# Splitting the next head's first weight block into halves across VectorE and SyncE, and reordering ScalarE and VectorE work in a hybrid decoder block

## What is computed

```python
# one chip core computes all of it; 528 tokens = 16 meta tokens + 512, width 1024, 8 heads of 128
u    = rmsnorm(h, norm_g)
proj = u @ w_in                                  # (528 x 1024) @ (1024 x 10240)
hq, hf, hi, hz, aq, ak, av, az, ga, gb = split(proj)
f    = lb + (1 - lb) * sigmoid(hf);  kA = 1 - f
oA   = hgrn2_chunked(hq, log(f), kA, hi)         # gated linear recurrence, per head
yA   = (rmsnorm(oA) * silu(hz)) @ w_branch_a
oB   = diff_attention(rope(aq), rope(ak), av, lam)  # two causal softmaxes, one subtracted, per head
yB   = (rmsnorm(oB) * (1 - lam_init) * silu(az)) @ w_branch_b
h    = h + (sigmoid(ga) * yA + sigmoid(gb) * yB) @ w_out
out  = rmsnorm(h, final_g)                       # the meta tokens dropped
```

## Time and profile before

| what | us |
|---|---|
| median of 3 runs (734.7 to 736.45) | 734.8 |
| the profiled execution's own time | 735.62 |
| span of the profiled execution | 733.7 |
| PE busy | 707.5 (96%) |
| DVE busy | 531.7 (72%) |
| ACT busy | 363.7 (50%) |
| POOL busy | 112.9 (15%) |

### The profile page before, as it was taken

One profiled execution on the slowest core, in us unless ns is written; L12 is line 12 of the kernel. 1 busy time (PEld: TensorE's weight loads), 2 busy tenths in 40 slices (PEclk: granted clock), 3 DMA queues, 4 the chain that ended last, 5 costly groups with the idle time before them and its releaser, 6 DMA issues.

```text
span 733.7 us, 14433 instructions
## 1 busy us (share of the span) xinstructions
PE 707.5 (96%) x4953; PEld 651.0 (89%) x4953; DVE 531.7 (72%) x1240; ACT 363.7 (50%) x739; POOL 112.9 (15%) x134
## 2 busy tenths in 40 slices
PE   2999999999999999999999999999999999999995
PEld 2998999999899899999989999989989988888884
DVE  4899878788768777878877877887688872735352
ACT  5454653655464565376455455536566562222232
POOL 2011211221121122121112112112111000000000
PEclk9999999999999999999999999999999999999998
DMA  7355545557546554655754755565677553325102
GB/s 271 115 130 130 130 130 157 130 114 179 107 114 186 129 129 130 162 126 119 177 111 107 194 117 131 144 156 132 143 201 201 188 175 111 99 102 201 58 14 102
DMA packets 36243, 101.86 MB, mean 139 GB/s; under 512 B 4050, under 2 KB 4452, under 8 KB 36212
## 3 DMA queue, kind: packets, MB, share of 16 engines
q1 hardware_dynamic: 21492, 68.29, 26.9%
q0 software_dynamic: 14400, 32.51, 25.4%
q10 hardware_dynamic: 320, 0.66, 0.3%
HBM read 66.84 MB, written 2.10 MB: 94 GB/s over the span
## 4 chain that ended last, share of the span: by engine, by line
PE 69%; issue 10%; DMA 8%; DVE 7%; ACT 2%; POOL 2%; DVEq 0%; SPq 0%; POOLq 0%; ACTq 0%
PE ps L655 20%; PE ps L656 19%; PE ps L657 19%; DMA w_raw<-w_raw 3%; PE ps L821 3%; DMA w_raw<-in_w_in 2%; PE ps L807 1%; PE ps L891 1%; DMA w_lo<-w_raw 1%; DVE w_lo L365 1%; PE ps L917 1%; DMA x_in<-in_x 1%; PE ps L837 1%; PE ps L908 1%; POOL small L609 1%
## 5 line engine op out<-in xcount | busy, mean ns | idle before, releaser
L655 PE MATMUL ps<-uT_hi,w_hi 128*128 128x272 f32 (+3 forms) x704 | 226.3, 321 | 2.0 <-ACT p L1133 1.8
L656 PE MATMUL ps<-uT_lo,w_hi 128*128 128x272 f32 (+3 forms) x704 | 215.4, 306 | 0.0
L657 PE MATMUL ps<-uT_hi,w_lo 128*128 128x272 f32 (+3 forms) x704 | 215.2, 306 | 0.0
L655 PEld LDWEIGHTS ps<-uT_hi,w_hi 128*128 128x128 f32 x704 | 133.2, 189 | 10.7 <-DVE w_lo L365 1.7
L657 PEld LDWEIGHTS ps<-uT_hi,w_lo 128*128 128x128 f32 x704 | 132.9, 189 | 5.9
L656 PEld LDWEIGHTS ps<-uT_lo,w_hi 128*128 128x128 f32 x704 | 133.2, 189 | 4.6
L655 PE MATMUL ps<-t_hi,w_hi 128*128 128x256 f32 x352 | 103.1, 293 | 0.0
L657 PE MATMUL ps<-t_hi,w_lo 128*128 128x256 f32 x352 | 99.5, 283 | 0.0
L656 PE MATMUL ps<-t_lo,w_hi 128*128 128x256 f32 x352 | 99.4, 282 | 0.0
L322 ACT ACTIVATE w_hi<-w_raw 128x1024 fp32r<-128x1024 f32 x53 | 56.1, 1060 | 81.2 <-PE ps L657 54.0
L358 ACT ACTIVATE w_hi<-w_raw 128x512 fp32r<-128x512 f32 x132 | 78.2, 623 | 24.8 <-DMA w_raw<-in_w_in 11.1
(11 more groups left out here) (240 smaller groups left out, 1436.2 us busy)
## 6 DMA issues: line engine op xcount, KB each, us to landing
w_raw<-in_w_in SPq DMA_DIRECT2D x78, 512.0 KB, 3.6
w_lo<-w_raw POOLq DMA_DIRECT2D x24, 512.0 KB, 4.8
w_lo<-w_raw POOLq DMA_DIRECT2D x32, 256.0 KB, 4.3
w_sum<-in_w_in SPq DMA_DIRECT2D x22, 256.0 KB, 3.0
w_sum<-w_raw POOLq DMA_DIRECT2D x22, 256.0 KB, 3.3
w_raw<-w_raw POOLq DMA_DIRECT2D x22, 256.0 KB, 4.3
w_raw<-in_w_branch_a SPq DMA_DIRECT2D x8, 512.0 KB, 3.5
w_raw<-in_w_branch_b SPq DMA_DIRECT2D x8, 512.0 KB, 3.3
```

The costliest lines, as they stand in the source:

```text
L655: pe.matmul(dst, w[0], rhs[0], start=start, stop=False, skip_group_check=True)
L656: pe.matmul(dst, w[0], rhs[1], start=False, stop=False, skip_group_check=True)
L657: return pe.matmul(dst, w[1], rhs[0], start=False, stop=stop, skip_group_check=True)
```

## The change

The arithmetic and its results stay; so does the number of products. Six things change.

1. SP loads the next head's HI in two halves of 256 KB. The first waits for the low part of part 5 (one less in `pair_lo`), the second for that of part 6, as the whole did. The first half has a semaphore of its own (`half_loaded`).
2. PE's unit HI waits at its start for the first half of its low part (`lo_first`) and for `comb` one lower (`sum_16` instead of `out_21`); at its second product group (k = 0, b = 1) for `out_21`; at k = 4 for the second half of the low part.
3. DVE does the second half of HI's low part behind `out_21`, not ahead of `norm`.
4. DVE does `masked(3)` right behind the low part of part 1, ahead of `out_12`, low part 2 and `sum_2`, and `probs(3)` ahead of `sum_4` and low part 5.
5. ACT does the exponentials of block 3 ahead of the high part of part 5; it saves parts 0 and 1 (`p_1`, `p_5`) ahead of part 6's high part, the tanh behind that; and it takes part 3's result (`c_11(1)`) ahead of `square`.
6. ACT takes HZ's gate (`take(h, 5)`) and rounds the rotated queries (`rotated_hi(h, 1)`) ahead of the high parts 0 and 3 of pair 0.

```diff
--- before.py
+++ after.py
@@ -233,10 +233,11 @@
     x_loaded = [sem(f"x_loaded{i}") for i in range(CH)]
     xres_loaded, stored = sem("xres_loaded"), sem("stored")
     w_loaded = [sem(f"w_loaded{i}") for i in range(2 * RAW)]
+    half_loaded = sem("half_loaded")
 
     slot_free = sem("slot_free")
     hi_ready, lo_ready, w_used = sem("hi_ready"), sem("lo_ready"), sem("w_used")
-    hi_first = sem("hi_first")
+    hi_first, lo_first = sem("hi_first"), sem("lo_first")
     sums, pair_hi, pair_lo = sem("sums"), sem("pair_hi"), sem("pair_lo")
     early_loaded, late_loaded = sem("early_loaded"), sem("late_loaded")
     base_loaded = [sem(f"base_loaded{i}") for i in range(2)]
@@ -330,7 +331,7 @@
 
     def half_hi(act, half, loads, free):
 
-        act.wait_ge(w_loaded[0], 16 * loads)
+        act.wait_ge((half_loaded, w_loaded[0])[half], 16 * loads)
         act.wait_ge(w_used, free)
         act.activation(blk(w_hi, half), w_raw[:, 0, half * BLK:(half + 1) * BLK], ACT.Copy)             .then_inc((hi_first, hi_ready)[half], 1)
 
@@ -339,8 +340,7 @@
         dve.wait_ge((hi_first, hi_ready)[half], ready)
         ins = dve.tensor_tensor(blk(w_lo, half), w_raw[:, 0, half * BLK:(half + 1) * BLK], blk(w_hi, half).bitcast(F32),
                                 ALU.subtract)
-        if half == 1:
-            ins.then_inc(lo_ready, 1)
+        ins.then_inc((lo_first, lo_ready)[half], 1)
 
     def part_hi(act, q, j, r, loads, i, free):
 
@@ -432,6 +432,12 @@
             def columns(h, col, r):
 
                 load(r, w_in[bass.ds(h + col // P, 1), :, :])
+
+            def half_columns(h, col, half):
+
+                cols = slice(half * BLK, (half + 1) * BLK)
+                return sp.dma_start(w_raw[:, 0, cols],
+                                    w_in[bass.ds(h + col // P, 1), :, cols].rearrange("u p n -> p (u n)"))
 
             def half_block(h, col, r, half):
 
@@ -502,9 +508,12 @@
                 units_of_head(h)
                 pair_of_head(h, 0, h + 1, PAIRS[0])
                 pair_of_head(h, 1, h + 1, PAIRS[1])
+                sp.wait_ge(pair_lo, LOWS * 2 * (h + 1) - 1)
+                sp.sem_inc(slot_free, 1)
+                half_columns(h + 1, HI, 0).then_inc(half_loaded, 16)
                 sp.wait_ge(pair_lo, LOWS * 2 * (h + 1))
                 sp.sem_inc(slot_free, 1)
-                columns(h + 1, HI, 0)
+                half_columns(h + 1, HI, 1).then_inc(w_loaded[0], 16)
                 sp.wait_ge(part_added[1], 32 * h + 32)
                 sp.sem_inc(slot_free, 1)
                 columns(h + 1, HZ, 1)
@@ -689,12 +698,14 @@
                     return tuple(backwards(a, k) for a in (uT_hi, uT_lo))
                 return tuple(a[:, k, META if s == 1 else 0:META + HALF] for a in (uT_hi, uT_lo))
 
-            def section(s, slot, ks):
+            def section(s, slot, ks, combined=None):
 
                 for k in ks:
                     w = tuple(a[:, slot, k * P:(k + 1) * P] for a in (w_hi, w_lo))
                     if s in (0, 1, 4):
                         for b in range(2):
+                            if (s, k, b) == (4, 0, 1):
+                                pe.wait_ge(comb, combined)
                             last = three(recurrent_out(s, b), w, recurrent_in(s, b, k), k == 0 and (s, b) != (1, 1),
                                          k == KT - 1)
                     elif s % 2 == 0:
@@ -709,19 +720,21 @@
 
             def unit(h, j, k):
 
+                if (j, k) == (0, KT // 2):
+                    pe.wait_ge(lo_ready, UNITS + h + 1)
                 if k == 0:
                     if j == 0:
-                        pe.wait_ge(lo_ready, UNITS + h + 1)
+                        pe.wait_ge(lo_first, h + 1)
                         pe.wait_ge(c11_taken, 2 * h + 2)
                     else:
                         pe.wait_ge(unit_added[j - 1], 16 * h + 16)
                     if j < 2:
-                        pe.wait_ge(comb, 10 * h + 8 + 2 * j)
+                        pe.wait_ge(comb, 10 * h + 7 + 3 * j)
                     elif j == 2:
                         pe.wait_ge(sec_taken, UNITS + 2 * h + 1)
                     else:
                         pe.wait_ge(gate_ready, 2 * h + 3)
-                section(4 + j, j, [k])
+                section(4 + j, j, [k], 10 * h + 8)
 
             def part(q, j, half, i, lo_done, meta):
 
@@ -1220,9 +1233,9 @@
                 rotated_hi(h, 0)
                 take(h, 4)
                 unit_hi(act, 1, UNITS * h + 4, 3, made(h - 1, 15), True)
-                parts(0, 0, 3)
                 take(h, 5)
                 rotated_hi(h, 1)
+                parts(0, 0, 3)
                 if isinstance(h, int) and h == 0:
                     t_high(2, t3_sum, 3)
                 exps(h, 0)
@@ -1247,25 +1260,26 @@
                 c_11(0)
                 parts(1, 0, 3)
                 probs_out(h, 2)
-                parts(1, 1, 2, 4, 5)
+                parts(1, 1, 2, 4)
                 exps(h, 3)
+                parts(1, 5)
+                p_1(1)
+                p_5(1)
+                parts(1, 6)
                 if last:
                     gate_rest(0, 2 * h)
                 else:
                     act.wait_ge(comb, 10 + 10 * h + 5)
                     act.activation(kk[:, META + HALF:], kk[:, META + HALF:], ACT.Tanh, scale=0.5).then_inc(k_tanh, 1)
-                p_1(1)
-                p_5(1)
-                parts(1, 6)
                 probs_out(h, 3)
+                c_11(1)
                 if last:
                     gate_hi(0, 0)
                 square(h, 1, B_A, at_done, atn(h, "a3"))
-                c_11(1)
                 if last:
                     gate_hi(0, 3, 1)
                 else:
-                    half_hi(act, 0, UNITS * h + 7, made(h, 16))
+                    half_hi(act, 0, h + 1, made(h, 16))
                     half_hi(act, 1, UNITS * h + 7, made(h, 17))
                     unit_hi(act, 1, UNITS * h + 7, 1, made(h, 19), True)
 
@@ -1489,6 +1503,8 @@
                 first_mark(ins)
                 dve.wait_ge(dve_own, first[0])
 
+            dve.wait_ge(lo_ready, UNITS + 1)
+            dve.sem_inc(lo_first, 1)
             opening(0, first_mark, first_chain)
             dve.sem_inc(dve_own, OWN - first[0])
 
@@ -1834,13 +1850,14 @@
                 sum_16(0)
                 out_21(0)
                 out_22(0)
-                low(1, 1, 2)
+                low(1, 1)
+                masked(3)
+                out_12(0)
+                low(1, 2)
                 sum_2(dve, 2 * h + 1, 0)
-                out_12(0)
-                masked(3)
+                probs(3)
                 sum_4(dve, 2 * h + 1, 0)
                 low(1, 5)
-                probs(3)
                 low(1, 6)
                 sum_75(1)
                 if not last:
@@ -1850,12 +1867,13 @@
                 norm_sum(1)
                 if not last:
                     half_lo(dve, 0, h + 1)
-                    half_lo(dve, 1, UNITS * h + UNITS + 5)
                 norm(1, B_A)
                 if last:
                     gate_low(0, 3, 1, 2)
                 sum_16(1)
                 out_21(1)
+                if not last:
+                    half_lo(dve, 1, UNITS * h + UNITS + 5)
                 out_22(1)
                 gated(1)
                 out_12(1)
```

## The result

The changed kernel takes 740.15 us (median of 5 runs, 739.26 to 742.33), against 734.8 us before (5 runs beside them, 734.29 to 736.45). The ratio is 1.0067, with a 95% interval from 1.0045 to 1.0088: slower by 5.4 us. The profiled span grew from 733.7 to 738.0 us. The forecast was 731.5 us with a range up to 738.0. Its sign was wrong, and the time lies outside its range.

A forecast was written before the change was run, and what follows sets the result against it. PE's idle time was taken to bound the kernel. Block 3 2.4 plus boundary 1.3 less 0.4 for late AV gave 3.3 us off the 734.8 median: 731.5 us, range 730.4 to 738.0.

The forecast's parts named there:

- What bounds the kernel: Whole kernel: TensorE is busy in 96% of the span, so only its idle time can be won.
- Block 3: Turned probabilities of query block 3: an earlier masked minimum removes PE's wait in the first seven heads, 2.4 us gained.
- Boundary: Start of the next head's unit HI: the relaxed wait removes 0.3 to 0.33 us at four boundaries, 1.3 us gained.
- AV's load: SP's queue: the load is issued 1.9 us later, behind HI's late second low half, while PE is 0.7 us earlier.
- the last term of AV's chain: AV's add, before unit AV: takes 4.8 us, chain done at 300.6 against 301.2 wanted; 0.4 us set for worse heads.
- rival 2: Unit AV: AV comes late at every head, 1.1 us in each of seven; slower, 738.8 us; chance 0.16.
- Rival 1: Unit HZ: AV's load slows HZ's add by 1.9 us, 0.4 behind PE, seven heads; 733.9 us; chance 0.22.
- Item 6: ScalarE's gate and rounded queries ahead of HF's high parts: nothing on the path, nothing gained, 0 us.
- Last head: Last head: its 0.7 us block 3 wait goes, but PE waits more for the gates' low part; 0 gained.
- Split load: HI's load in halves on SP: one more DMA, 0.33 us each, same bytes; worth nothing by itself.

The follow-up runs named there:

- one-line experiment: Changed kernel with VectorE doing the second half of HI's low part ahead of the norm again (item 3 undone): 731.81 us against 734.96 before the change, ratio 0.9963.

## Why the prediction was wrong

**What bounds the kernel: right.** PE's idle time set the time, before and after.

**Block 3: right in kind, somewhat less in size.** The wait went in every head, and PE's starts gain 2.1 us by it in the first seven, forecast 2.4. Against PE's transposes the exponentials come 1.0 us earlier (276.69 where PE asks at 280.52; before 276.68 and 279.55), and not 1.4, because the masked minimum now waits for PE's scores of that block. `probs(3)` ends 1.0 us ahead of PE, the room that was forecast.

**Boundary: right, in size too.** 2.63 to 2.69 us from turn to first level, forecast 2.64; the seven stretches took 19.93 us before and take 18.62 now, the 1.3 of the forecast. From the start of the first half to the norm it is 1.61 us, before 1.62: taking the second half away did not bring the norm forward. The one-line experiment does without item 3 and has no wait there either, so the relaxed `comb` is what counts, as the prediction said. In the whole time it is worth about 0.6 us by the ratios of the kernels with and without it (0.9963 and 0.9971, intervals overlapping), 1.1 by the waits.

**AV's load: right in place and delay.** Forecast 1.9 us later with PE 0.7 earlier. Measured against the attention's turn, it went from 0.95 ahead (286.11 and 287.06) to 1.27 behind (289.26 and 287.99): 2.2 us. Of the 0.7, 0.35 lies ahead of the turn, so the forecast comes to 2.25 by this measure.

**The step that failed** is the last term of AV's chain: "AZ's load waits for HZ's add, so it is issued near 294, some 2 us ahead of AV's add at 295.8, and is mostly through", by which AV's add was put at its price alone, 4.8 us, and the chain at 0.4 us in all. It took 7.87. Two inputs of that sentence were off. HZ's add was put at 4.8 to 5.5 us and took 6.40, since AV's load started with it; so AZ's load came late by the same. And AV's load, put at 5.2 us, took 4.00, so AV's add came early. The gap of 2 us closed from both sides, to 0.06. By the seven heads a start some tenths of a us earlier or later would not have kept it open, since both of its ends hang by the end of AV's load. Measured on the new timeline, an add of 4.8 would have ended at 300.7, and PE wanted it at 302.67 (303.63 less 0.96): 2 us of room in place of a wait of 1. The term, 0.4, measured 8.9 us by the waits of the weight loads and 7.9 by PE's starts.

The argument behind it, "the bytes that slow one transfer cannot slow the next as well", is wrong as it stood against rival 2. Each collision is a new one, of other bytes: AV's load with HZ's add, then AZ's load with AV's add. I had the row that shows the price, 7.67 us where AZ's load followed 0.50 behind the earlier trace rows, and used it as the far end instead of asking from which offset on it holds. The head that I priced was also the most favourable but one. In the kernel before AV's add took 6.5 to 7.7 us in four of the last seven heads, with AZ's load 0.50 to 0.74 behind it; 5.5 to 5.6 in two, 1.3 to 1.5 behind; and 4.86 in the last, 2.07 behind. **Rival 2**, with a chance of 0.16, is what happened: slow add, wait at the first product of unit AV in seven heads, and its price of 1.1 us a head is the 1.13 of the rows. Its time was 738.8; it had no wait at unit HZ. It put the load at 5.2 and the add at 6.5 where 4.0 and 7.9 were measured, so its size is partly luck.

**Rival 1** forecast HZ's add slowed by 1.9; it was slowed by 1.63 and cost PE a wait in one head of seven. The Trainium skill, "DMA: Bandwidth & Descriptors", on queues, rings and completion order, has each DMA engine take turns between its queues packet by packet. The trace does not show such turns where the two start together: both lose (the add 4.77 to 6.40, the load 3.3 to 4.0 us), but the add's packets hold back until most of the load's are through, as the fences of the result show for AV's add.

**Item 6: wrong, though unseen in the result.** "Nothing on the path, nothing gained either" was true of the kernel before and false of the kernel that the change makes. It is the cover of the late AV load, and 37 us lie under it. The prediction named the mechanism ("in the old ACT order the gate and the rounded queries would queue behind them") and did not price it.

**Last head: right.** The wait for the gates' low part is 1.72 us, before 1.73; nothing was won there.

**Split load (item 1).** No experiment took it alone. The one-line experiment has it and shows no wait for it.

## What to carry to other kernels

When an edit moves one load later, do not price the transfers behind it each at its time alone: draw where each load and each add starts against the other, and look at what sets each start. Here a load and an add that start together release a load and an add that start together again, so the collision comes twice. And ask of every row that sets a price how the same row reads in the other heads. An order that "gains nothing" today may be what keeps a late transfer from stopping the tensor engine; price it in the changed schedule, with the transfers as late as they will be. And try the parts of a change one by one: here five of six parts were good for 0.4% and the sixth cost 1%.

## What was not expected of the hardware

- A 512 KB add from SBUF into SBUF, issued by GpSimd, took 4.72 us with no load beside it, 6.4 us with a 512 KB load that started with it, 6.7 with 512 KB at AV's place, and 7.50 to 7.96 with 768 KB. A load of 512 KB beside it took 4.0 us, and 3.3 alone. In heads 1 to 6 of the five kernels whose AV load goes early, AV's add took 7.5 to 8.0 us where AZ's load was issued 0.31 to 0.52 us behind it, 6.5 to 6.8 where it was 0.54 to 0.74, and 5.3 to 5.7 where it was 0.94 to 1.70. The Trainium skill, "DMA: Bandwidth & Descriptors", gives a fit of 2.0 us and bytes over 436 GB/s for one DMA issued by GpSimd, by which 512 KB would take an estimated 3.2 us: the loads on SP's queue come near to it, the adds do not.
- A wait of 4 us on PE was followed by 3.3 us at the lower granted clock (0.50), and such waits cost some 1.9 us each on top of themselves; with waits of 1.4 us or less in its heads, the changed kernel's mean clock was 0.996.
